# Second even attention of a two-block model: its outputs in one PSUM bank, and a third out-projection unit beside its steps

## What is computed

```python
def _even_mixer(x, norm_g, w_in, qn_a, kn_a, sink_a, qn_b, kn_b, rpb_b, w_out):
    h = _rmsnorm(x, norm_g)
    qa, ka, va, qb, kb, vb = _split(h @ w_in, EVEN_SPLITS)
    ...
    oa = _window_gqa(qa, ka, va, sink_a)
    ...
    ob = _neighbourhood_attn(qb, kb, vb, rpb_b)
    return jnp.concatenate([oa, ob], axis=-1) @ w_out
```

## Time and profile before

| | us |
|---|---|
| median of 3 runs (2220.94 to 2223.43) | 2222.04 |
| the profiled execution, its own time | 2224.77 |
| the profiled execution, span of the core | 2222.9 |
| PE busy in the span | 2161.4 |
| DVE / ACT / POOL busy | 1052.1 / 853.4 / 883.6 |
| the second attention begins (scores of item 0) | 985.63 |
| its last values product begins | 1047.28 |
| unit 4 of the out-projection begins | 1059.48 |

### The profile page before, as it was taken

One profiled execution on the slowest core, in us unless ns is written; L12 is line 12 of the kernel. 1 busy time (PEld: TensorE's weight loads), 2 busy tenths in 40 slices (PEclk: granted clock), 3 DMA queues, 4 the chain that ended last, 5 costly groups with the idle time before them and its releaser, 6 DMA issues.

```text
span 2222.9 us, 28163 instructions
## 1 busy us (share of the span) xinstructions
PE 2161.4 (97%) x10402; PEld 1735.7 (78%) x10402; DVE 1052.1 (47%) x1527; ACT 853.4 (38%) x1281; POOL 883.6 (40%) x682
## 2 busy tenths in 40 slices
PE   6999999899999989999999999999999999999999
PEld 5875688678888868766788888888888877888887
DVE  5765646676626253466541322436743756423121
ACT  6434544532222242455442332434433344423231
POOL 3521235144444444210544444343343325444443
PEclk9999999999999999999999999999999999999999
DMA  4222123123333242110332223322222212332233
GB/s 154 76 67 76 48 76 105 48 85 115 112 98 101 95 138 81 52 35 19 99 101 96 95 95 100 114 79 76 76 86 76 76 48 97 102 96 95 95 99 100
DMA packets 54970, 193.41 MB, mean 87 GB/s; under 512 B 6096, under 2 KB 6352, under 8 KB 54480
## 3 DMA queue, kind: packets, MB, share of 16 engines
q1 hardware_dynamic: 50400, 181.58, 24.9%
q10 hardware_dynamic: 4464, 10.36, 1.4%
HBM read 189.82 MB, written 2.10 MB: 86 GB/s over the span
## 4 chain that ended last, share of the span: by engine, by line
issue 54%; POOL 28%; PE 17%; POOLq 1%; ACT 0%; DMA 0%; DVE 0%; SPq 0%; DVEq 0%; ACTq 0%
POOL wl L511 28%; PE gemm_ps L542 6%; PE gemm_ps L543 6%; PE gemm_ps L544 6%; POOLq L508 0%; POOLq L516 0%; DMA con<-con_in 0%; ACT xh L1334 0%; ACT wh L1311 0%; ACT sq L1341 0%; DVE tmp L1941 0%; ACT L1318 0%; DVE xl L1871 0%; PE turn_ps L633 0%; DVE x L1967 0%
## 5 line engine op out<-in xcount | busy, mean ns | idle before, releaser
L511 POOL TENSOR_TENSOR wl<-raw,wh 128x512 fp32r<-128x512 f32 x678 | 883.4, 1326 | 1321.6 <-ACT wh L1311 1321.4
L1311 ACT ACTIVATE wh<-raw 128x1024 fp32r<-128x1024 f32 x339 | 359.0, 1059 | 765.9 <-DMA raw<-w_in 751.0
L542 PE MATMUL gemm_ps<-xh,wh 128*128 128x512 f32 x1352 | 543.8, 402 | 30.2 <-DVE xl L1871 14.9
L544 PE MATMUL gemm_ps<-xh,wl 128*128 128x512 f32 x1352 | 530.0, 392 | 0.0
L543 PE MATMUL gemm_ps<-xl,wh 128*128 128x512 f32 x1352 | 530.0, 392 | 0.0
L543 PE MATMUL gemm_ps<-arena_r,wh 128*128 128x512 f32 (+1 forms) x1088 | 417.1, 383 | 0.0
L542 PEld LDWEIGHTS gemm_ps<-xh,wh 128*128 128x128 f32 x1352 | 256.0, 189 | 98.4 <-issue 28.0
L542 PE MATMUL gemm_ps<-arena_r,wh 128*128 128x512 f32 (+1 forms) x832 | 320.1, 385 | 1.4 <-POOL wl L511 0.8
L544 PE MATMUL gemm_ps<-arena_r,wl 128*128 128x512 f32 (+1 forms) x832 | 317.5, 382 | 0.0
L543 PEld LDWEIGHTS gemm_ps<-xl,wh 128*128 128x128 f32 x1352 | 256.2, 189 | 56.4 <-issue 4.8
L544 PEld LDWEIGHTS gemm_ps<-xh,wl 128*128 128x128 f32 x1352 | 255.8, 189 | 54.2
(11 more groups left out here) (383 smaller groups left out, 2354.1 us busy)
## 6 DMA issues: line engine op xcount, KB each, us to landing
raw<-w_in SPq DMA_DIRECT2D x339, 512.0 KB, 3.4
arena<-na_in ACTq DMA_DIRECT2D x14, 256.0 KB, 2.7
x<-x_in SPq DMA_DIRECT2D x8, 256.0 KB, 6.7
out<-x ACTq DMA_DIRECT2D x8, 256.0 KB, 2.7
arena<-alibi_in ACTq DMA_DIRECT2D x6, 256.0 KB, 3.5
con<-con_in SPq DMA_DIRECT2D x1, 1432.0 KB, 11.6
arena<-moba_in ACTq DMA_DIRECT2D x1, 1024.0 KB, 4.8
arena<-mem_in ACTq DMA_DIRECT2D x1, 1024.0 KB, 4.9
```

Source lines behind the costliest of these rows:

```text
L511: m = pool.tensor_tensor(wl[:, k, half], raw[:, k, half], wh[:, k, half].bitcast(F32), ALU.subtract)
L542: pe.matmul(o, wh[:, n % RING, w], h[:, kt, 0:width], start=(kt == 0), stop=False)
L544: last = pe.matmul(o, wl[:, n % RING, w], h[:, kt, 0:width], start=False, stop=(kt == nkt - 1))
L1311: act.activation(wh[:, k % RING, :], raw[:, k % RING, :], ACT.Copy).then_inc(high_split, 1)
```

## The change

All four groups of the second attention write bank 0 of `out_ps` (`single=True`). So the first item of groups 1, 2 and 3 waits until the group just before has been read by ACT and DVE. In the steps of these items (7, 11 and 15) its values product goes behind the turning and the pieces of the step. The freed bank 1 takes unit 2 of the out-projection, whose triples are spread over the steps, and unit 3 alone is left in a bank of the scores. Ahead of the last values product (that of item 15, in step 18) stood 18 triples of the out-projection, 14 of units 0 and 1 and 4 of unit 2; now there are 21, the same 14 and 7 of unit 2. After the steps 7 triples are left of units 0 to 3 (1, 1, 1 and 4) where there were 10.

```diff
-        OUT_PIECES = {4: [(1, 0, 2)], 5: [(0, 0, 2)], 7: [(1, 2, 4)], 9: [(0, 2, 4)], 11: [(1, 4, 5)], 12: [(0, 4, 5)],
-                      13: [(1, 5, 6)], 14: [(0, 5, 6)], 16: [(1, 6, 7)], 17: [(0, 6, 7), (2, 0, 4)], 18: [(3, 0, 4)]}
-
-        out_banks = (gemm_ps[:, 1, :], gemm_ps[:, 0, :], score_ps[:, 0, :], score_ps[:, 1, :])
+        OUT_PIECES = {4: [(1, 0, 2)], 5: [(0, 0, 2)], 6: [(2, 0, 2)], 7: [(1, 2, 4)], 8: [(2, 2, 4)], 9: [(0, 2, 4)],
+                      11: [(1, 4, 5)], 12: [(0, 4, 5)], 13: [(2, 4, 5)], 14: [(1, 5, 6), (0, 5, 6)], 15: [(2, 5, 6)],
+                      16: [(1, 6, 7)], 17: [(0, 6, 7), (2, 6, 7)], 18: [(3, 0, 4)]}
+
+        out_banks = (gemm_ps[:, 1, :], gemm_ps[:, 0, :], out_ps[:, 1, :], score_ps[:, 1, :])
...
                 def values(i, it):
+
                     if it["first"] and groups0 + it["group"] >= 2:
-                        pe.wait_ge(group_used, groups0 + it["group"] - 1)
+                        pe.wait_ge(group_used, groups0 + it["group"] - (0 if single and it["group"] else 1))
                     chunks = it["nk"] // P
                     for c in range(chunks):
                         for s in range(2):
-                            o = out_ps[s * HD:(s + 1) * HD, it["group"] % 2, it["tile"] * P:(it["tile"] + 1) * P]
+                            o = out_ps[s * HD:(s + 1) * HD, 0 if single else it["group"] % 2, it["tile"] * P:(it["tile"] + 1) * P]
...
                     if i < n:
                         scores(i, items[i])
+                    late = single and i >= 3 and items[i - 3]["first"] and items[i - 3]["group"]
                     if i >= 3:
                         take(probs_copied)
-                        values(i - 3, items[i - 3])
+                        if not late:
+                            values(i - 3, items[i - 3])
                     if 2 <= i < n + 2:
                         turned(i - 2, items[i - 2])
                     between(i)
+                    if late:
+                        values(i - 3, items[i - 3])
...
-                        if i == 17:
+                        if i == 18:
 
                             pe.wait_ge(scores_used, taken[scores_used] + 1)
...
-            pair_attention(pair_items("neighbour"), window_part)
+            pair_attention(pair_items("neighbour"), window_part, single=True)
             blocks_split[0] += 4
             pe.wait_ge(group_used, outputs0 + 4)
             for u in range(4):
-                piece(even_out + u, out_banks[u], 7 if u < 2 else 4, KT, xh, xl)
+                piece(even_out + u, out_banks[u], 7 if u < 3 else 4, KT, xh, xl)
```

More of the change, by code:

```diff
@@ L755, in cross_attention, with pair_attention @@
                 taken[group_used] = groups0 + 4
-            def pair_attention(items, between=lambda i: None, wide=False):
+            def pair_attention(items, between=lambda i: None, wide=False, single=False):
                 groups0 = taken.get(group_used, 0)
@@ L1407, in cross_attention, with pair_attention @@
                 taken[item_done] = items0 + n
-            def pair_attention(items, whole=False, between=lambda i: None, wide=False):
+            def pair_attention(items, whole=False, between=lambda i: None, wide=False, single=False):
                 items0 = taken.get(item_done, 0)
@@ L1436, in outputs @@
                         return
-                    o, a = xh[:, it["to"], :], out_ps[:, it["group"] % 2, :]
+                    o, a = xh[:, it["to"], :], out_ps[:, 0 if single else it["group"] % 2, :]
                     if it["turned"]:
@@ L1802, in window_part @@
                     raise_to(even_out + 3)
-            pair_attention(pair_items("neighbour"), between=window_part)
+            pair_attention(pair_items("neighbour"), between=window_part, single=True)
             prepare(x, "mlp0", mh, stored(FIRST["even_out"]), adds=KT - 1)
@@ L2007, in cross_attention, with pair_attention @@
                 take(probs_turned, 3)
-            def pair_attention(items, between=lambda i: None, whole=False, wide=False):
+            def pair_attention(items, between=lambda i: None, whole=False, wide=False, single=False):
                 def logits(i, it):
@@ L2041, in outputs @@
                         return
-                    h, l, a = xh[:, it["to"], :], xl[:, it["to"], :], out_ps[:, it["group"] % 2, :]
+                    h, l, a = xh[:, it["to"], :], xl[:, it["to"], :], out_ps[:, 0 if single else it["group"] % 2, :]
                     if it["turned"]:
@@ L2486, in split_window @@
                          rhs_ready)
-            pair_attention(pair_items("neighbour"), split_window)
+            pair_attention(pair_items("neighbour"), split_window, single=True)
             add(even_out, "mlp0", mh, ml, lambda n0, b: out_banks[b] if b < 4 else gemm_ps[:, (n0 + b) % 2, :],
```

## The result

Five runs of the changed kernel take 2229.99 to 2237.21 us, median **2236.01 us**; the kernel before, in five runs beside it, has the median 2222.04. The ratio is 1.0056 with a 95% interval of 1.0045 to 1.0068, so slower by 10 to 15 us. The profiled execution took 2235.89 us with a span of 2234.0.

A forecast was written before the change was run, and what follows sets the result against it. PE's waits were taken to bound the kernel: 7.0 us of chain (0.65 + 3.3 + 2.8 + 0.3) plus 6.0 of clock make 13.0 us, so 2235 us as a median, range 2228 to 2240 us.

The forecast's parts named there:

- The chain: Second attention: late values products wait for ACT and DVE to read the bank, delaying what is queued behind; 7.0 us.
- +0.65: Start of second attention to the end of DVE's first low half: two unit 2 triples in step 6 delay it, us.
- +3.3: From the end of DVE's first low half to its second: products, scores, turning and triples queue behind the wait, us.
- +2.8: From the end of DVE's second low half to its third: late products, scores, turning and triples add this, us.
- +0.3: From the end of DVE's third low half to the last values product: fewer triples, more products and turning, us.
- The tail gives nothing back: After the steps: unit 4 hangs on unit 0's last triple by 8.7 us, so fewer triples only lengthen PE's wait.
- The clock: Four longer PE waits bring stretches at half clock, 1.65 us each at 0.9 of the places; 6 us.
- The chain alone: Second attention: same seven microseconds, no or one stretch at half clock; +7 to +8.7, 2229 to 2231 us; chance 0.21.
- "Filling works": Steps: bank read early enough, so added triples fill PE's idle time; -1.9 us, 2220 us; chance 0.03.
- "Absorbed": Steps: slack on PE, DVE and ACT shrinks the late product's delay; +1 to +4 us, 2223 to 2226; chance 0.07.
- "Long stretches behind two or more": PE's long waits: 6.5 us at half clock behind two or more; +17 to +20 us, 2239 to 2242; chance 0.11.
- the main case: PE's four long waits: two to four short stretches at half clock, +10 to +15 us in all; chance 0.58.

The follow-up runs named there:

- the run with repeated triples: Changed kernel with 18 out-projection triples done again in PE's four long waits, to keep PE busy: 2228.41 us, ratio 1.0030 to the kernel before.
- the old table: Changed kernel with the earlier table of pieces and earlier banks of units 2 and 3, no third unit beside the steps: 2234.23 us, ratio 1.0055.
- the place alone: Kernel before with only the values products of steps 7, 11 and 15 moved behind turning and piece, two banks kept: 2223.36 us, ratio 1.0005.
- the moved end of the table: Kernel before with unit 2's first four triples behind the last values product and unit 3 whole at the end: 2220.82 us, ratio 0.9991.
- the first four experiments: Values products moved alone; one bank without third unit; repeated triples; finished group read early with two banks. The kernel before beside them: median 2222.17 us.

## Why the prediction was right

- **The bound.** PE's waits decide, and the same work stands in a longer span: shown.
- **The chain.** Forecast +0.65, +3.3, +2.8 and +0.3, sum 7.0. Without the clock's share the run with repeated triples gives +3.36, +2.78 and +0.10. For the first part the traces of before and after can't be compared, as the kernel before had its long stretch at half clock there and the changed one had none. Pairs in the same state of the clock give +0.33 (the changed kernel against the old table, both without a stretch) and +0.38 (repeated triples against the place alone, both with a short one). So the chain cost about 6.6 us, and the term of +0.65 was about twice too large.
- **The tail gives nothing back.** Unit 4 began 8.72 us after unit 0's last triple in both kernels; the run with the old table says the same with three more triples between, and the moved end of the table shows the other side: what moves unit 0's last triple moves unit 4.
- **The clock.** Forecast were four waits with stretches at half clock at 0.9 of them, 1.65 us each, 6 us. All four had one, but two were long (some 6.8 us, at the first and the last wait), and the share was 8.2 us: this term was mis-sized, 2.2 too little. I took the short stretch for the likeliest everywhere. Against that stands 0.7 us which nobody forecast: the kernel before had a long stretch in the first part (30.21 us), the changed one none (29.51 with the old table and no stretch). So the stage's 14.1 us are 6.6 of chain and 8.2 of clock at the waits, less 0.7; that 13.0 came so near is in part the luck of errors that cancel. The prediction also called 1.94 us a wait that sufficed, and passed over its own: the long stretch there follows a wait of only 1.53 us. The rule of the Trainium skill ("TensorE: Matmul & The Clock Gate", "HAM oscillation — how this bites in real kernels"), that bursts behind waits start cold, agrees with the traces for the waits of 2.5 us or more, each of which had a stretch at half clock; for shorter ones the traces go both ways.
- **The rivals.** The chain alone, 2229 to 2231 us, is close to what the run with repeated triples has (2228.41). "Filling works" needed an earlier release; given one, it did work in the steps, and won nothing over two banks. "Absorbed" is ruled out by the release distances. "Long stretches behind two or more" is what the profile shows, two of them, but not at its price of +17 to +20 us: the two cost 2.9 and 2.7 us, not 3.25, in part because they began within the wait, and the short ones 1.5 and 1.2. What happened lies between the main case, which had short stretches only, and this rival.
- **What isn't shown:** that the half clock always follows such waits. The changed kernel's fastest run, 2229.99 us, had a mean granted clock of 0.991 where the four others had 0.986 or 0.987, so it had less time at half clock; which stretches it lacked has no trace.

## What to carry to other kernels

Before a buffer is taken from a pair to make room for more filler work, look up when the remaining one is released, on the engines that read it, and what stands in the in-order queue behind the new wait; here the wait was 3 us, and each release came later by the time of the products, scores and triples that stood behind it (+3.4 and +2.8 us); putting one set of scores ahead of the wait took 0.9 us off. Filler work pays only where it shortens what the next dependency hangs on: here unit 4's weights hung on unit 0's last triple, and work should have been kept for that wait, not taken from it (keeping more there made the stage 2.0 us shorter). A wait of 2.5 us or more on TensorE cost more than its length here (1.2 to 2.9 us more each, in clock); repeating harmless matmuls in it is a cheap way to measure that.

## What was unexpected of the hardware

Doing 18 triples (54 matmuls) more made the changed kernel 7.6 us faster, since the granted clock stayed at full. The wait of 1.5 us before the scores of item 3 had a stretch at half clock behind it in eight of ten profiles, not in the changed kernel's nor with the old table, and one of 1.89 us had none; waits of 2.5 us or more had one in each case looked at here (eleven in four kernels). The wait of 1.5 us in the timeline of PE of the kernel before, just ahead of the long stretch of the earlier trace rows:

```profile
994.20 0.70 PE L765 MATMUL score_ps<-arena 64*128 64x256 f32 x4 [1.53 <-DVE small L2017]
```

A wait of 1.97 us ahead of the attention had one in seven of the ten, for example in the kernel before (275.3 to 278.8) and not in the changed one.

The same instructions ahead of the attention ended between 982.68 and 986.90 us in ten profiles. Nearly all of the 2.95 us between the kernel before and the changed one arises in one place: the same matmul starts at 139.79 and 139.69 us, and a later one at 199.24 and 196.45. In between the kernel before had a stretch at half clock from about 138.8 to 145.6 that the changed one had not, although no wait shortly before it was longer than 1.03 us. First the kernel before, then the changed one, from the view by stretches:

```profile
142.00:145.00 3.00, 3.00 (x8) 2.32 (x9) 2.90 (x4) 0.00 (x0) 1.79 (x2) 0.50 0.01 3
142.00:144.00 2.00, 2.00 (x10) 1.62 (x10) 1.97 (x2) 0.00 (x0) 1.72 (x2) 1.00 0.01 4
```

The two profiles that started the attention next soonest, at 983.45 and 984.19, had a short stretch at that place, the seven others a long one. The times of the whole runs go with the mean granted clock too: beside the first four experiments the kernel before took 2226.35 us at 0.988 and 2217.81 at 0.994. So this kernel's medians carry a few microseconds of where the half clock fell, and a stage cut at the same instructions carries less, but not nothing, as its first part shows.
